# Wider pieces of the expert gate and up weights: 4 contraction blocks by 512 columns

## The chip, the cores and the metric

One core of a Trainium2 chip runs the whole program. The metric is device time in microseconds (us), the median of several runs; lower is better. All data is float32. TensorE does the matmuls, VectorE (DVE) and ScalarE (ACT) work on tiles, GpSimd (POOL) does little here, and SyncE (SP) issues nearly all loads.

## The reference

A decoder of two layers over 256 tokens of width 1024. What matters here is the second layer's mixture of experts, 8 experts of inner width 2816, two chosen for each token:

```python
def swiglu(h, w_gate, w_up, w_down):
    return (jax.nn.silu(h @ w_gate) * (h @ w_up)) @ w_down

def moe_ffn(h, w_router, w_gate, w_up, w_down):
    ...
    logits = (hf @ w_router).astype(jnp.float32)
    top_vals, top_idx = lax.top_k(logits, TOP_K)
    top_w = jax.nn.softmax(top_vals, axis=-1)
    gates = jnp.einsum('nk,nke->ne', top_w, jax.nn.one_hot(top_idx, N_EXPERTS, dtype=jnp.float32))
    out = jnp.zeros_like(hf)
    for e in range(N_EXPERTS):
        out = out + gates[:, e:e + 1].astype(hf.dtype) * swiglu(hf, w_gate[e], w_up[e], w_down[e])
    return out.reshape(B, S, D)
```

Before it stand, in each layer, a norm, an input projection, three groups of token mixers and an output projection; the first layer has one dense SwiGLU of the same inner width. A last norm closes the trunk.

## The kernel before

**Precision.** A float32 operand is split into a high part (`hi`, what ScalarE's copy to the matmul type keeps) and a low part (`lo`, the rest, by a subtraction on VectorE). A product is three matmuls, high by high, high by low, low by high: `mm3`, lines 1394 to 1398, which is why nearly every matmul of the profile stands at L1396, L1397 or L1398.

**Pieces.** All large weights pass in pieces of 1 MB, 128 partitions by 2048 numbers (`PIECE`). SyncE loads a piece into a raw slot. ScalarE writes its high part into `hi_ring` and VectorE its low part into `lo_ring`; both rings have three slots (`SPLIT`). In the expert part there are 11 raw slots: `raw_a` (4) and `raw_m` (7). Semaphores tie them: a raw slot is loaded again when its low part is made (`lo_ready`), a ring slot is written again when TensorE has used the piece before in it (`piece_used`), and TensorE waits for `lo_ready` ahead of each piece.

**Items.** An expert is an item; with up to 128 tokens each, 8 to 11 items run (here 8; the first is written out, the rest are a loop). `gather` (L1678) brings the item's tokens, transposed, into `sel_hi` and `sel_lo` (parts of the tiles `hT_hi` and `hT_lo`) by matmuls with a one-hot matrix. Then 33 pieces follow in the order `ORDER` (lines 116 to 125): G0 U0, then for strips 1 to 10 Gc Uc D(c-1), and D10 last. A strip is `FC` = 256 of the 2816 inner columns. A gate (G) or up (U) piece holds all 8 contraction blocks (`KT`) by 256 columns: 24 matmuls with 128x128 of the tokens stationary and 128x256 of weights moving. Gate and up of a strip share one PSUM bank, `bank[c % 2]`, a half each:

```python
o = bank[c % 2][:, 0:FC] if kind == "G" else bank[c % 2][:, FC:2 * FC]
for k in range(KT):
    ...
    r = mm3(o, sel_hi[:, k, :], sel_lo[:, k, :], wh[:, k, :], wl[:, k, :], k == 0, k == KT - 1)
```

A down (D) piece is 2 contraction blocks by 1024 columns: 12 matmuls with 512 moving columns into banks 4 and 5, which accumulate over the whole item.

**Between them.** After Uc ScalarE makes `m_sg` = Silu of the gate half (L895) and VectorE `m_prod` = up times `m_sg` (L1356). Behind G(c+1) TensorE transposes the two blocks of `m_prod` (`transpose_act`, L1698) into bank 2 or 3; ScalarE copies them to `m_hi` (L905), VectorE makes `m_lo` (L1361), and D(c) uses both. The last strip's transposes stand behind D9, ahead of the next item's gather.

**Order on ScalarE and VectorE.** Their loop `item` goes over the pieces j = 0 to 32: first the split of piece j+2 (`split_expert`, L631 and L935), then what belongs to piece j. At an item's end ScalarE copies banks 4 and 5 to `y_hi` (L910) and VectorE makes `y_lo` (L1379). The next item adds this to `x`: `scatter` (L1690, L1691, four matmuls each behind U0 and behind G1) and `scatter_add` on VectorE (L1340, two each). The one-hot matrix of the current item is transposed behind G2 (L1735).

## Time and profile before

| | |
|---|---|
| median of 3 runs | 1342.34 us (1341.87 to 1343.02) |
| span of the profiled execution | 1337.6 us |
| between the span and the median | 4.7 us |
| TensorE busy | 1278.1 us, 96% |
| VectorE, ScalarE busy | 1022.3 us (76%), 832.6 us (62%) |
| read from HBM | 342.67 MB |

The profile is one execution. Its span runs from the first to the last instruction; for the profiled execution itself no other time is listed, so the time around the span is taken from the median. The expert part begins with the first gather at 503 us and goes on to the end. Times in rows are microseconds from the span's start, unless marked ns. PE is TensorE, PEld its loads of the stationary operand. Matmuls are pipelined, so one matmul's duration is longer than the distance from its start to the next one's: the distance is what the stream costs.

### The profile page before, as it was taken

The page shows a single profiled execution, that of the slowest core. Times are in us where ns is not written, and L with a number is a line of the kernel's source. Part 1 is how long each engine was busy: PE and PEld are TensorE (multiplying, and loading weights), DVE is VectorE, ACT ScalarE, POOL GpSimd, SP SyncE. Part 2 cuts the span into 40 slices and gives each one's busy share as a digit, 9 for nine tenths or more (in the row PEclk, how much of TensorE's full clock was granted, in tenths as well). Part 3 has the DMA queues.
Part 4 walks back from the last instruction along what each step waited for, and adds up shares of the span by engine and source line. Part 5 has one row for each costly group of instructions (what it writes and reads, how often), then busy time and mean ns, then how long its engine had stood idle before and what let it go on. Part 6 is the DMA issues. An engine that isn't in the chain of part 4 may idle for free.

```text
span 1337.6 us, 22912 instructions
## 1 busy us (share of the span) xinstructions
PE 1278.1 (96%) x8754; PEld 1170.5 (88%) x8754; DVE 1022.3 (76%) x1163; ACT 832.6 (62%) x957; POOL 117.4 (9%) x121
## 2 busy tenths in 40 slices
PE   6898899999899789999999999999999999999997
PEld 6876799999787669999999999999999999999996
DVE  5885654455598658888888888888888888888885
ACT  5356544444545656777776776776776777776774
POOL 2850000000086010000000000000000000000000
PEclk9889999999998988999999999999999999999998
DMA  9400665556442069999999999999999999999960
GB/s 326 157 5 1 229 197 183 185 188 189 138 127 71 1 212 366 357 361 304 355 359 307 354 363 299 359 356 306 352 360 303 355 352 320 344 349 324 344 209 31
DMA packets 256650, 344.47 MB, mean 258 GB/s; under 512 B 5558, under 2 KB 227316, under 8 KB 256596
## 3 DMA queue, kind: packets, MB, share of 16 engines
q1 hardware_dynamic: 255772, 341.27, 76.2%
q0 software_dynamic: 624, 1.93, 0.4%
q8 instruction: 35, 0.57, 0.2%
q10 hardware_dynamic: 200, 0.54, 0.1%
q14 instruction: 19, 0.16, 0.0%
HBM read 342.67 MB, written 1.05 MB: 257 GB/s over the span
## 4 chain that ended last, share of the span: by engine, by line
PE 87%; DVE 7%; ACT 3%; issue 2%; DMA 0%; SPq 0%; POOL 0%; POOLq 0%; DVEq 0%; ACTq 0%
PE bank L1396 26%; PE bank L1398 26%; PE bank L1397 26%; PE bank L1678 3%; PE bank L1698 1%; DVE cv L1051 1%; PE bank L1493 1%; DVE lo_ring L930 1%; DVE xn L1051 1%; PE bank L1690 1%; ACT hi_ring L625 1%; PE bank L1691 1%; PE bank L1533 1%; DVE s_sb L1109 0%; DVE q_m L1084 0%
## 5 line engine op out<-in xcount | busy, mean ns | idle before, releaser
L1396 PE MATMUL bank<-hi_ring,hT_hi 128*128 128x256 f32 (+2 forms) x1536 | 449.4, 293 | 0.0
L1397 PE MATMUL bank<-lo_ring,hT_hi 128*128 128x256 f32 (+2 forms) x1536 | 440.7, 287 | 0.0
L1398 PE MATMUL bank<-hi_ring,hT_lo 128*128 128x256 f32 (+2 forms) x1536 | 440.7, 287 | 0.0
L935 DVE TENSOR_TENSOR lo_ring<-raw_m,hi_ring 128x2048 fp32r<-128x2048 f32 x168 | 384.3, 2291 | 60.0 <-ACT hi_ring L631 59.5
L631 ACT ACTIVATE hi_ring<-raw_m 128x2048 fp32r<-128x2048 f32 x168 | 321.0, 1911 | 26.3 <-PE bank L1398 26.3
L1396 PEld LDWEIGHTS bank<-hi_ring,hT_hi 128*128 128x128 f32 x1536 | 293.6, 191 | 8.1 <-issue 1.3
L1397 PEld LDWEIGHTS bank<-lo_ring,hT_hi 128*128 128x128 f32 x1536 | 293.8, 191 | 7.3 <-issue 0.5
L1398 PEld LDWEIGHTS bank<-hi_ring,hT_lo 128*128 128x128 f32 x1536 | 293.7, 191 | 2.7
L935 DVE TENSOR_TENSOR lo_ring<-raw_a,hi_ring 128x2048 fp32r<-128x2048 f32 x96 | 219.4, 2292 | 40.1 <-ACT hi_ring L631 40.1
L930 DVE TENSOR_TENSOR lo_ring<-raw_a,hi_ring 128x2048 fp32r<-128x2048 f32 (+2 forms) x59 | 131.8, 2236 | 93.8 <-ACT hi_ring L625 93.7
L631 ACT ACTIVATE hi_ring<-raw_a 128x2048 fp32r<-128x2048 f32 x96 | 183.4, 1911 | 16.3 <-PE bank L1398 16.3
L1396 PE MATMUL bank<-hT_hi,hi_ring 128*128 128x256 f32 (+1 forms) x576 | 165.2, 287 | 2.2 <-DVE hT_lo L965 2.2
L1397 PE MATMUL bank<-hT_lo,hi_ring 128*128 128x256 f32 (+1 forms) x576 | 163.7, 284 | 0.0
L1398 PE MATMUL bank<-hT_hi,lo_ring 128*128 128x256 f32 (+1 forms) x576 | 163.7, 284 | 0.0
L625 ACT ACTIVATE hi_ring<-raw_a 128x2048 fp32r<-128x2048 f32 (+2 forms) x59 | 109.9, 1863 | 68.9 <-PE bank L1398 62.5
L1396 PE MATMUL bank<-hi_ring,m_hi 128*128 128x512 f32 x352 | 139.4, 396 | 0.0
L1397 PE MATMUL bank<-lo_ring,m_hi 128*128 128x512 f32 x352 | 139.0, 395 | 0.0
L1398 PE MATMUL bank<-hi_ring,m_lo 128*128 128x512 f32 x352 | 139.0, 395 | 0.0
L1396 PEld LDWEIGHTS bank<-hT_hi,hi_ring 128*128 128x128 f32 (+1 forms) x576 | 110.2, 191 | 3.2 <-issue 2.6
L1397 PEld LDWEIGHTS bank<-hT_lo,hi_ring 128*128 128x128 f32 (+1 forms) x576 | 110.3, 191 | 0.5
L1398 PEld LDWEIGHTS bank<-hT_hi,lo_ring 128*128 128x128 f32 (+1 forms) x576 | 110.1, 191 | 0.0
L554 POOL TENSOR_TENSOR rstd<-ms,half_neg 128x1 f32<-128x1 f32 x10 | 6.0, 600 | 1159.4 <-DVE ms L940 1159.4
(266 smaller groups left out, 1457.8 us busy)
## 6 DMA issues: line engine op xcount, KB each, us to landing
raw_m<-in_w_down_exp SPq DMA_DIRECT2D x64, 1024.0 KB, 6.0
raw_m<-in_w_up_exp SPq DMA_DIRECT2D x56, 1024.0 KB, 6.6
raw_m<-in_w_gate_exp SPq DMA_DIRECT2D x48, 1024.0 KB, 5.6
raw_a<-in_w_gate_exp SPq DMA_DIRECT2D x40, 1024.0 KB, 6.4
raw_a<-in_w_up_exp SPq DMA_DIRECT2D x32, 1024.0 KB, 6.8
raw_a<-in_w_down_exp SPq DMA_DIRECT2D x24, 1024.0 KB, 5.2
raw_a<-in_w_in SPq DMA_DIRECT2D x12, 1024.0 KB, 7.1
raw_a<-in_w_gate_dense SPq DMA_DIRECT2D x11, 1024.0 KB, 5.4
```

Of the source, the lines that this page charges most:

```text
L625: A(hi_of(n)[:, 0:w], t[:, 0:w], ACT.Copy).then_inc(hi_ready, 1)
L631: A(hi_of(NA + j), t, ACT.Copy).then_inc(hi_ready, 1)
L930: V.tensor_tensor(lo_of(n)[:, 0:w], raw_slot(n)[0][:, 0:w], hi_of(n)[:, 0:w].bitcast(F32), ALU.subtract).then_inc(lo_ready, 1)
L935: V.tensor_tensor(lo_of(NA + j), expert_slot(i, j)[0], hi_of(NA + j).bitcast(F32), ALU.subtract).then_inc(lo_ready, 1)
L1051: conv(V.scalar_tensor_tensor(out, win, wc, old, ALU.mult, ALU.add))
L1396: M(o, lh, rh, start=start, stop=False)
L1397: M(o, lh, rl, start=False, stop=False)
L1398: return M(o, ll, rh, start=False, stop=stop)
L1493: r = M(bank[1 + r3][0:QD, hh * T:(hh + 1) * T], w_uq[:, c, h * QD:(h + 1) * QD], cq[:, c, :], start=c == 0, stop=c == 1)
L1533: r = nc.tensor.transpose(bank[T_BANK[k % 2]][:, b * P:(b + 1) * P], e_sb[:, k % 3, 0, b * P:(b + 1) * P], ident)
L1678: r = M(bank[b0 + h][:, kk * P:(kk + 1) * P], src[:, t, k * P:(k + 1) * P], onehot[:, t, :], start=t == 0, stop=t == TT - 1)
L1690: M(b[:], onehot_t[:, t, :], y_hi[:, n * 512:(n + 1) * 512], start=True, stop=False)
```

## The change

The expert part gets an order and a strip width of its own. A strip is `EW` = 512 columns, so there are `EC` = 6 strips, five of 512 and one of 256 (2816 = 5 x 512 + 256). A gate or up piece of a 512 strip holds 4 of the 8 contraction blocks by 512 columns; a strip has two of each (`part` 0 and 1), which accumulate into the same bank. The last strip's gate and up are one piece each, with 8 blocks by 256 columns as before. A down piece keeps its form; a 512 strip has two. There are 33 pieces of 1 MB as before, in the order G0 G0 U0 U0, then G G U U D D for strips 1 to 4, then G5 U5 D4 D4 D5. A gate or up piece of a 512 strip is loaded in rows of 2 KB, half as many as before.

Gate goes to bank 0 and up to bank 1, for every strip. The next strip's gate waits for the Silu of this one, its up for the product. Silu stands behind the last gate piece instead of behind the up piece. `m_sg` and `m_prod` have one buffer each, 512 wide, in the tile `xn`, which is free then. Transposes, their copy and their low part are four blocks at a time. The four scatter matmuls that stood behind U0 and behind G1 stand behind the first piece of each, the one-hot transposes behind the first piece of U2, and VectorE makes the next one-hot matrix behind the first piece of D2 instead of behind U5.

```diff
+EW = 2 * FC
+EC = (FF + EW - 1) // EW
...
+    def up(kind, c):
+        return [(kind, c, part) for part in range(expert_width(c) // FC)]
+
+    def down(c):
+        return [("D", c, part) for part in range(expert_width(c) // FC)]
+
+    order = up("G", 0) + up("U", 0)
+    for c in range(1, EC):
+        order += up("G", c) + up("U", c) + down(c - 1)
+    return order + down(EC - 1)
...
-        m_sg = sb("m_sg", [P, 2, FC])
-        m_prod = sb("m_prod", [P, 2, FC])
-        m_hi = sb("m_hi", [P, 2, 2, P], F32R)
-        m_lo = sb("m_lo", [P, 2, 2, P], F32R)
+        m_hi = sb("m_hi", [P, 2, 4, P], F32R)
+        m_lo = sb("m_lo", [P, 2, 4, P], F32R)
...
+        m_sg, m_prod = spare[:, 0:EW], spare[:, EW:2 * EW]
...
-                        src = w[one, :, c * FC:(c + 1) * FC].rearrange("e (k p) n -> p (e k) n", p=P)
-                    sp.dma_start(ff_view(t, kind), src).then_inc(s, 16)
+                        rows = PIECE // expert_width(c) * P
+                        src = w[one, part * rows:(part + 1) * rows, c * EW:c * EW + expert_width(c)
+                                ].rearrange("e (k p) n -> p (e k) n", p=P)
+                    sp.dma_start(expert_view(t, kind, c), src).then_inc(s, 16)
...
-                    if kind == "U":
-                        act.wait_ge(piece_used, expert_done(i, "U", c))
-                        act.wait_ge(prod_done, GU0 + c - 1 + i * NCH)
-                        A(m_sg[:, c % 2, :], bank[c % 2][:, 0:FC], ACT.Silu).then_inc(sg_done, 1)
+                    w = expert_width(c)
+                    if kind == "G" and last_part(kind, c, part):
+                        act.wait_ge(piece_used, expert_done(i, "G", c))
+                        act.wait_ge(prod_done, GU0 + c + i * EC)
+                        A(m_sg[:, 0:w], bank[0][:, 0:w], ACT.Silu).then_inc(sg_done, 1)
...
-                        if c >= 2:
-                            dve.wait_ge(act_t, c - 1 + i * NCH)
-                        V.tensor_tensor(m_prod[:, c % 2, :], bank[c % 2][:, FC:2 * FC], m_sg[:, c % 2, :],
-                                        ALU.mult).then_inc(prod_done, 1)
+                    if kind == "U" and last_part(kind, c, part):
+                        dve.wait_ge(sg_done, GU0 + c + 1 + i * EC)
+                        dve.wait_ge(piece_used, expert_done(i, "U", c))
+                        dve.wait_ge(act_t, c + i * EC)
+                        V.tensor_tensor(m_prod[:, 0:w], bank[1][:, 0:w], m_sg[:, 0:w], ALU.mult).then_inc(prod_done, 1)
...
-                        if kind == "G" and c >= 2:
-                            pe.wait_ge(prod_done, GU0 + c - 1 + i * NCH)
-                        o = bank[c % 2][:, 0:FC] if kind == "G" else bank[c % 2][:, FC:2 * FC]
-                        for k in range(KT):
+                        if part == 0 and c >= 1:
+                            if kind == "G":
+                                pe.wait_ge(sg_done, GU0 + c + i * EC)
+                            else:
+                                pe.wait_ge(prod_done, GU0 + c + i * EC)
+                        o = bank[0 if kind == "G" else 1][:, 0:w]
+                        for kk in range(PIECE // w):
+                            k = part * (PIECE // w) + kk
...
-                    if kind == "G" and c >= 1:
+                    if kind == "G" and c >= 1 and last_part(kind, c, part):
                         transpose_act(i, c - 1)
-                    if not first and c <= 1 and kind == ("U", "G")[c]:
+                    if not first and c <= 1 and kind == ("U", "G")[c] and part == 0:
                         scatter(i, 2 * c)
                         scatter(i, 2 * c + 1)
```

How the rows stand on two engines. First ScalarE in the first item (its loop over the pieces), before: a bit more than one strip. L631 is the split of a weight piece, L895 Silu, L905 the copy of the transposes.

```order
L631 ACTIVATE hi_ring<-raw_a 128x2048 [waits piece_used,raw_in0]
L905 ACTIVATE m_hi<-bank 128x256 [waits piece_used,act_t]
L631 ACTIVATE hi_ring<-raw_a 128x2048 [waits piece_used,raw_in1]
L895 ACTIVATE m_sg<-bank 128x256 [waits prod_done,piece_used]
L631 ACTIVATE hi_ring<-raw_a 128x2048 [waits piece_used,raw_in2]
L631 ACTIVATE hi_ring<-raw_a 128x2048 [waits piece_used,raw_in3]
L905 ACTIVATE m_hi<-bank 128x256 [waits piece_used,act_t]
L631 ACTIVATE hi_ring<-raw_m 128x2048 [waits piece_used,raw_in4]
L895 ACTIVATE m_sg<-bank 128x256 [waits prod_done,piece_used]
```

The same engine with the change, one strip of the first item; L664 is the split, L929 Silu (it writes into `xn`), L940 the copy.

```order
L664 ACTIVATE hi_ring<-raw_m 128x2048 [waits piece_used,raw_in8]
L929 ACTIVATE xn<-bank 128x512 [waits prod_done,piece_used]
L940 ACTIVATE m_hi<-bank 128x512 [waits piece_used,act_t]
L664 ACTIVATE hi_ring<-raw_m 128x2048 [waits piece_used,raw_in9]
L664 ACTIVATE hi_ring<-raw_m 128x2048 [waits piece_used,raw_in10]
L664 ACTIVATE hi_ring<-raw_a 128x2048 [waits piece_used,raw_in0]
L664 ACTIVATE hi_ring<-raw_a 128x2048 [waits piece_used,raw_in1]
L664 ACTIVATE hi_ring<-raw_a 128x2048 [waits piece_used,raw_in2]
L664 ACTIVATE hi_ring<-raw_a 128x2048 [waits piece_used,raw_in3]
L929 ACTIVATE xn<-bank 128x512 [waits prod_done,piece_used]
```

Silu and the copy, which alternated between splits, now stand together, once in six splits, and are twice as wide. Second TensorE in the loop, before: the last matmuls of U0, the scatter, the first of G1.

```order
L1396 MATMUL bank<-hi_ring,hT_hi 128x256
L1397 MATMUL bank<-lo_ring,hT_hi 128x256
L1398 MATMUL bank<-hi_ring,hT_lo 128x256
L1690 MATMUL bank<-hT_hi,onehot_t 128x512 [waits ylo_done0]
L1691 MATMUL bank<-hT_lo,onehot_t 128x512
L1690 MATMUL bank<-hT_hi,onehot_t 128x512 [waits ylo_done1]
L1691 MATMUL bank<-hT_lo,onehot_t 128x512
L1704 REGISTER_ALU
L1396 MATMUL bank<-hi_ring,hT_hi 128x256 [waits lo_ready]
```

With the change: the last matmuls of the first piece of U0, the scatter, the first of its second piece.

```order
L1432 MATMUL bank<-hi_ring,hT_hi 128x512
L1433 MATMUL bank<-lo_ring,hT_hi 128x512
L1434 MATMUL bank<-hi_ring,hT_lo 128x512
L1726 MATMUL bank<-hT_hi,onehot_t 128x512 [waits ylo_done0]
L1727 MATMUL bank<-hT_lo,onehot_t 128x512
L1726 MATMUL bank<-hT_hi,onehot_t 128x512 [waits ylo_done1]
L1727 MATMUL bank<-hT_lo,onehot_t 128x512
L1739 REGISTER_ALU
L1432 MATMUL bank<-hi_ring,hT_hi 128x512 [waits lo_ready]
```

The scatter stood behind two pieces of the item and now stands behind three; the matmuls around it are twice as wide and half as many.

## Rows read from the trace of the kernel before

**Rows 1.** The page: busy time by engine; granted TensorE clock in 40 slices

```profile
PE 1278.1 (96%) x8754; PEld 1170.5 (88%) x8754; DVE 1022.3 (76%) x1163; ACT 832.6 (62%) x957; POOL 117.4 (9%) x121
...
PEclk9889999999998988999999999999999999999998
```

**Rows 2.** Waits, 500 to 1330 us: waiter <- releaser: us, times, longest

```profile
DVE lo_ring L935 <- ACT hi_ring L631: 99.6, 216, 1.2
ACT m_hi L905 <- PE bank L1698: 95.0, 80, 2.6
...
PE bank L1663 <- DVE chosen L1279: 2.3, 1, 2.3
...
PE bank L1690 <- DVE hT_lo L1379: 1.4, 1, 1.4
```

**Rows 3.** Windows: length, busy us by engine, clock, DMA share, GB/s

```profile
620.00:700.00 80.00, 80.00 (x567) 74.88 (x566) 70.03 (x53) 56.91 (x46) 0.00 (x0) 1.00 1.04 352
604.55:706.52 101.97, 101.97 (x725) 95.53 (x724) 87.01 (x66) 72.41 (x62) 0.00 (x0) 1.00 1.01 340
706.52:808.49 101.97, 101.97 (x726) 95.53 (x724) 87.13 (x66) 72.40 (x62) 0.00 (x0) 1.00 1.01 341
```

**Rows 4.** Order of time, TensorE at an item's start: start, us, engine, line

```profile
713.11 0.28 PE L1396 MATMUL bank<-hi_ring,hT_hi 128*128 128x256 f32 x1
...
718.86 0.40 PE L1690 MATMUL bank<-hT_hi,onehot_t 128*128 128x512 f32 x1
...
719.79 0.28 PE L1396 MATMUL bank<-hi_ring,hT_hi 128*128 128x256 f32 x1
```

**Rows 5.** Order of time, TensorE in two strips: transposes, a down piece, transposes

```profile
700.64 0.38 PE L1698 MATMUL bank<-consts,m_prod 128*128 128x128 f32 x2
...
700.98 0.28 PE L1397 MATMUL bank<-lo_ring,hT_hi 128*128 128x256 f32 x1
...
703.72 0.39 PE L1396 MATMUL bank<-hi_ring,m_hi 128*128 128x512 f32 x1
...
706.52 0.38 PE L1698 MATMUL bank<-consts,m_prod 128*128 128x128 f32 x2
```

**Rows 6.** Order of time, TensorE in a down piece of the dense layer

```profile
301.92 0.39 PE L1396 MATMUL bank<-hi_ring,d_hi 128*128 128x512 f32 x1
...
305.81 0.39 PE L1398 MATMUL bank<-hi_ring,d_lo 128*128 128x512 f32 x1
```

**Rows 7.** Groups by line and form, 500 to 1330 us: busy us, mean ns

```profile
L935 DVE TENSOR_TENSOR lo_ring<-raw_m,hi_ring 128x2048 fp32r<-128x2048 f32 x168 | 384.3, 2291 | 60.0 <-ACT hi_ring L631 59.5
L631 ACT ACTIVATE hi_ring<-raw_m 128x2048 fp32r<-128x2048 f32 x168 | 321.0, 1911 | 26.3 <-PE bank L1398 26.3
...
L1356 DVE TENSOR_TENSOR m_prod<-bank,m_sg 128x256 f32<-128x256 f32 x88 | 36.8, 418 | 0.0
...
L1379 DVE TENSOR_TENSOR hT_lo<-bank,hT_hi 128x512 fp32r<-128x512 f32 x16 | 10.3, 686 | 23.6 <-ACT hT_hi L910 23.6
...
L910 ACT ACTIVATE hT_hi<-bank 128x512 fp32r<-128x512 f32 x16 | 8.7, 596 | 17.9 <-PE bank L1398 17.9
```

**Rows 8.** Order of time, ScalarE and VectorE at the same item's start

```profile
714.28 3.82 ACT L631 ACTIVATE hi_ring<-raw_a 128x2048 fp32r<-128x2048 f32 x2
...
716.22 4.49 DVE L935 TENSOR_TENSOR lo_ring<-raw_a,hi_ring 128x2048 fp32r<-128x2048 f32 x2 [1.00 <-ACT hi_ring L631]
...
719.14 0.39 ACT L895 ACTIVATE m_sg<-bank 128x256 f32<-128x256 f32 x1 [1.04 <-PE bank L1398]
```

**Rows 9.** Loads issued from 620 to 640 us: count, KB, us to landing

```profile
raw_m<-in_w_gate_exp SPq DMA_DIRECT2D x2, 1024.0 KB, 5.8
```

**Rows 10.** Loads issued from 680 to 700 us

```profile
raw_m<-in_w_gate_exp SPq DMA_DIRECT2D x2, 1024.0 KB, 7.5
```

More of the change, by code:

```diff
@@ L504, in expert_loads @@
             def expert_loads(e, i, first):
-                for j, (kind, c) in enumerate(ORDER):
+                for j, (kind, c, part) in enumerate(E_ORDER):
                     if first and j < RAW_A:
@@ L884, in item @@
             def item(i, more):
-                for j, (kind, c) in enumerate(ORDER):
+                for j, (kind, c, part) in enumerate(E_ORDER):
                     if j + 2 < NFF or more is True:
@@ L1343, in item @@
             def item(i, more, first=False):
-                for j, (kind, c) in enumerate(ORDER):
+                for j, (kind, c, part) in enumerate(E_ORDER):
                     if j + 2 < NFF or more is True:
@@ L1724, in item @@
                                 pe.wait_ge(gathered, 3 + k // 4 + 4 * i)
-                            r = mm3(o, sel_hi[:, k, :], sel_lo[:, k, :], wh[:, k, :], wl[:, k, :], k == 0, k == KT - 1)
+                            r = mm3(o, sel_hi[:, k, :], sel_lo[:, k, :], wh[:, kk, :], wl[:, kk, :],
+                                    k == 0, k == KT - 1)
                     r.then_inc(piece_used, 1)
-                    if kind == "G" and c >= 1:
+                    if kind == "G" and c >= 1 and last_part(kind, c, part):
@@ L1728, in item @@
                         transpose_act(i, c - 1)
-                    if not first and c <= 1 and kind == ("U", "G")[c]:
+                    if not first and c <= 1 and kind == ("U", "G")[c] and part == 0:
                         scatter(i, 2 * c)
                         scatter(i, 2 * c + 1)
-                    if kind == "G" and c == 2:
+                    if kind == "U" and c == 2 and part == 0:
                         pe.wait_ge(x_upd, XU0 + 4 * i)
```

69 lines of the change are left out of this document (41 added, 28 removed).

## The prediction, made before the changed kernel ran

> **What bounds the kernel now.** I read the engine line of the profile's page first, then the waits of the expert part, then the windows of single items, and last the order of time inside one item. The engine line has TensorE busy for 96% of the span, and the clock line shows full speed nearly everywhere from the middle on [rows 1]. In the waits of the expert part TensorE hardly appears: its longest are 2.3 us once at the routing and 1.4 us once at a scatter, while VectorE and ScalarE wait a hundred times for ScalarE and for TensorE [rows 2]. The two windows, each cut from the transposes of an item's last strip to the same place one item later, are 101.97 us long both times, with TensorE busy for all of it at clock 1.00 [rows 3]. So the eight items cost what the matmul stream costs, and everything else has to stay ahead of it. The reader should see that "busy" alone would not prove this; the absence of waits and the even pitch of the rows do.
>
> The stream's pitch is in the order of time. Gate and up of a first strip are 48 matmuls of 256 columns from 713.11 to 718.86: 5.75 us, 0.1198 us each, 2.875 us a piece [rows 4]. A down piece is 12 matmuls of 512 columns from 703.72 to 706.52: 2.80 us, 0.2333 us each [rows 5]. Two transposes take 0.22 us: from 700.64 to 700.98 there are 0.34 us, in which one 0.12 us matmul lies too [rows 5]. I check this against the window: 22 x 2.875 + 11 x 2.80 + 11 x 0.22 = 96.5, and 5.5 us remain for 32 gather matmuls, 8 scatter matmuls (0.93 us per four [rows 4]) and the one-hot transposes. It closes.
>
> **The change, part by part.** (1) *Wider matmuls.* In an item 20 of the 22 gate and up pieces change from 24 matmuls of 256 columns to 12 of 512; the last strip is 256 wide, and its two pieces keep their shape. The new form is that of the down pieces: moving rows of 512 from a ring slot, a 128x128 stationary operand, a whole bank written. So a piece falls from 2.875 to 2.80 us: 0.075 x 20 = 1.5 us an item, 8 items in this run, 12.0 us. Nothing overlaps this, since it is the stream that sets the end. The lower end of the price is the same 512 form in the dense layer, 17 matmuls from 301.92 to 305.81, 0.2288 us each [rows 6]: a piece would be 2.746 us, and the gain 0.129 x 160 = 20.6 us. The upper end is twice the 256 pitch, no gain. I take 0.2333, since it was measured in this loop, at its load of DMA.
>
> On what the pitch is made of: from the two rows, 2 x 0.1198 - 0.2333 = 6.3 ns are won for each pair of matmuls joined. The Trainium skill, "TensorE: Matmul & The Clock Gate", section "Back-to-back issue gap", gives an isolated warm gap of columns over 2.4 GHz plus 2.5 ns. By that rule a joined pair would win only 2.5 ns, 4.8 us in all (an estimate from the page); the rows of this trace stand at twice that, and the sum goes by the rows. The same section has about 131 ns for 512 columns in a stream with weight loads; the row's 233 ns disagree, and the measurement decides.
>
> (2) *Transposes.* Ten strips had two transposes each, behind the next strip's gate piece, and the eleventh two before the gather; now five strips have four each and the sixth two: 22 in both. At 0.11 us each nothing changes [rows 5].
>
> (3) *ScalarE and VectorE.* Of Silu, product and the two splits of the activation there are 6 each instead of 11, five of them twice as wide. A 256-wide one is 0.42 us on VectorE, a 512-wide one 0.69 (the y split has that form); the 512-wide ScalarE copy is 0.60 [rows 7]. Over an item VectorE has 22 x 0.42 = 9.2 us of them before and 10 x 0.69 + 2 x 0.42 = 7.7 after, ScalarE 22 x 0.39 [rows 8] = 8.6 before and 10 x 0.60 + 2 x 0.39 = 6.8 after. Neither is on the path, so this gives 0, but where the wide ones stand matters.
>
> (4) *The ring.* The ring of split weights has three slots. The split of piece j+2 can begin when piece j-1 is used; it takes 1.91 us on ScalarE, then 2.29 on VectorE [rows 7], and must be there 5.6 us after piece j started. The tightest place of a strip is behind the second gate piece, where Silu (moved here from behind the up piece) and the copy of the four transposes now follow each other. With 0 at the end of that piece's stream: Silu starts at 0.28 (719.14 against 718.86 [rows 4, 8]) and ends at 0.9, the copy ends at 1.5, the weight split on ScalarE runs to 3.4, that on VectorE to 5.7; VectorE's own low part of the activation fits between. The piece is due at 0.44 + 2 x 2.80 = 6.04, so 0.3 us are left. At the item's start the third piece is due at 713.11 + 5.60 = 718.71, since the scatter that stood before it is now behind it; VectorE ended the first of its two splits at 716.22 + 2.29 = 718.51 [rows 8]: 0.2 us left. The scatter's two additions on VectorE now stand behind the split of piece 4, and piece 4 is due after 4 x 2.80 + 0.93 us; 1 us and more is left there. So the ring costs 0 in the forecast, with 0 to 0.1 us an item as its bound at the item's start.
>
> (5) *Single banks.* Gate always goes to bank 0 and up to bank 1, and each new strip waits for the Silu and the product of the last. Silu ends 0.9 us behind gate, and the next gate begins more than 11 us behind it. The product follows the last up piece by a VectorE split at most (some 3 us), and the next up strip begins four pieces later. What queues behind these waits on TensorE is the whole stream, but they are met long before: 0. The product is also due at the next transposes, two down and two gate pieces later instead of one and one.
>
> (6) *Loads.* A gate or up megabyte is 512 rows of 2 KB instead of 1,024 of 1 KB; issues and slots stay. DMA has some share in this: between 620 and 700 us its engines are busy for 1.04 and move 352 GB/s [rows 3], while a gate load's time to landing grows from 5.8 to 7.5 us within the item [rows 9, 10]. So it falls behind a little in the strips and catches up in the gather. A slot is loaded 11 pieces ahead and split 2 ahead of use, some 9 x 2.9 = 26 us after its issue, which covers 7.5. At 352 GB/s 33 pieces need 98.3 us, less than the 100.5 us of a new item. The gain of longer rows falls where nothing waits: 0.
>
> **Sum.** An item goes from 101.97 to 100.45 us; 8 x 1.5 = 12.0. From this I take 0.3 us for the first microseconds of item 0 at the low clock and small stalls: 11.7. The span of 1337.6 us goes to 1325.9. What lies between the span and the median of the runs, 4.7 us, stays: 1330.6 us.
>
> **Rivals.** *The dense pitch* (0.2288 us): 1342.3 - 20.6 = 1321.7. For it, the same form shows it; against it, the loop's own rows do not, not even at the busiest or the quietest place. *Half the gain*: the 6.3 ns of a joined pair compare two kinds of piece with different stationary operands, so part of them may belong to the down piece and not to the width. With 3.2 ns a pair, 240 pairs an item and 8 items, 6 us are won: 1336.4. For it, each row is one kind only; against it, both pitches hold evenly over whole pieces. The rule of the Trainium skill quoted above ("TensorE: Matmul & The Clock Gate") would put the time at 1337.5, an estimate from the page. *DMA becomes the bound*: if what DMA moved in an item (340 GB/s [rows 3]) were all it could move, the item would stay at 101.97 us and the time at 1342. Against it speaks the 352 GB/s of the strips and the lag that is made up. *The ring falls behind*, the one that ends slower: behind the second gate piece VectorE delivers the split later than I work out, because Silu, copy and low part are wider. Its price is 40 strips times what exceeds 0.3 us. If each 512-wide operation took twice a 256-wide one, the 0.3 would just be used up, 1331; at 0.6 us late the gain is gone; at 0.8 us late it is 40 x 0.5 - 11.7 = +8, 1350.6. For it speaks that VectorE is busy for 87 of 102 us; against it, that the 512-wide rows are measured.
>
> **Chances.** The forecast 0.69; the dense pitch 0.12; half the gain 0.08; DMA 0.04; the ring 0.07. The range takes in the forecast, most of the dense pitch and half the gain, and leaves out the ring and DMA: 1322 to 1337. A measurement of this kernel can tell about 0.2%, 2.7 us, from no change. Faster by more than that: forecast, dense pitch and nearly all of the half gain, 0.88; same 0.05 (DMA and the rest of it); slower 0.07.
>
> **What would show it.** Right: gate and up rows of 128x512 at a start-to-start of 0.233 us; an item window of 100.4 to 100.5 us with TensorE busy throughout; no row in which TensorE waits for the low ring; loads landing sooner than 7.5 us late in an item. The ring's slip would show as TensorE idle before the first down piece of each strip with VectorE's split as releaser, and as VectorE no longer waiting for ScalarE. DMA as the bound would show as ScalarE waiting for a raw slot. A pitch of 0.229 us would mean the dense price. I am wrong if the 512 form with this stationary operand has another pitch than the down pieces, or if the split durations grow.

## The result, and the profile after

| | median | runs | lowest, highest |
|---|---|---|---|
| before | 1342.11 us | 4 | 1339.68, 1343.02 |
| changed | 1321.09 us | 4 | 1318.69, 1321.78 |

The ratio is 0.9846, with an interval of 0.9834 to 0.9858. The change wins 21.0 us where the forecast had 11.7, and the time lies 0.9 us below the lower end of the range. The profiled execution of the changed kernel took 1321.78 us with a span of 1320.0, so 1.8 us lie around the span. The page of the changed kernel, its span, its engine line, its clock line and its DMA line, to be read beside [rows 1]:

```profile
span 1320.0 us, 18637 instructions
PE 1260.0 (95%) x6834; PEld 1070.5 (81%) x6834; DVE 1011.0 (77%) x1083; ACT 828.8 (63%) x877; POOL 117.7 (9%) x121
...
PEclk9899999999899797999999999999999999999998
...
DMA packets 174725, 344.40 MB, mean 261 GB/s; under 512 B 5558, under 2 KB 63476, under 8 KB 174676
```

TensorE has 1920 matmuls fewer (240 an item, 8 items) and is still the engine that is always busy. Windows of the changed kernel, columns as in [rows 3]: the same 80 us, and two items, cut from gather to gather.

```profile
620.00:700.00 80.00, 80.00 (x385) 66.53 (x384) 71.20 (x46) 57.88 (x39) 0.00 (x0) 1.00 1.00 359
604.77:704.30 99.53, 99.53 (x487) 82.88 (x486) 85.75 (x56) 71.95 (x52) 0.00 (x0) 1.00 0.97 349
704.30:803.76 99.46, 99.46 (x487) 82.88 (x486) 85.68 (x56) 71.92 (x52) 0.00 (x0) 1.00 0.97 349
```

An item went from 101.97 to 99.46 us, 2.51 less, where 1.5 was forecast. TensorE fills it as before, at clock 1.00. From the first gather to the last the stretch went from 815.35 to 796.54 us, 18.8 less: seven items at 2.5, and the first, which begins at a lower clock, at 1.3 (101.58 to 100.28). The two executions differ in how long that clock lasted; the window from 511 to 515 us, columns as in [rows 3], before and after:

```profile
511.00:515.00 4.00, 4.00 (x31) 4.00 (x31) 2.84 (x12) 2.46 (x2) 0.00 (x0) 0.85 1.06 367
```

```profile
511.00:515.00 4.00, 4.00 (x12) 3.23 (x12) 2.85 (x36) 2.40 (x2) 0.00 (x0) 0.50 1.05 387
```

The granted clock was 0.50 from 502.0 to 512.2 us before and from 502.3 to 516.0 us after, so 9.1 us of the first item passed at it before and 11.5 us after; at half the clock 2.4 us more cost 1.2 us (an estimate from these rows), which is what the first item gained less. What stands ahead of the first gather was 1.4 us longer in this execution (504.49 against 503.11) and the tail 0.2 shorter, so the span is 17.6 us shorter than the span shown before.

The pitch, in the changed kernel's order of time on TensorE (columns as in [rows 4]): two gate or up pieces and two down pieces.

```profile
675.43 0.39 PE L1432 MATMUL bank<-hi_ring,hT_hi 128*128 128x512 f32 x1
676.11 0.39 PE L1432 MATMUL bank<-hi_ring,hT_hi 128*128 128x512 f32 x1
...
680.88 0.60 PE L1734 MATMUL bank<-consts,xn 128*128 128x128 f32 x4
681.23 0.48 PE L1432 MATMUL bank<-hi_ring,hT_hi 128*128 128x512 f32 x1
...
686.80 0.39 PE L1432 MATMUL bank<-hi_ring,m_hi 128*128 128x512 f32 x1
...
692.39 0.28 PE L1432 MATMUL bank<-hi_ring,hT_hi 128*128 128x256 f32 x1
```

This is the surprise. From 675.43 to 680.88 there are 24 matmuls with `hT_hi` and `hT_lo` as the stationary operand: 5.45 us, **0.2271 us** each. From 686.80 to 692.39 there are 24 of the same form, same ring, same 512 columns, with `m_hi` and `m_lo`: 5.59 us, **0.2329 us** each. So [rows 5] gave the right price for the down pieces, and the wrong one for the pieces that the change made. [rows 5] and [rows 6] were not all that the trace of the kernel before had on this form. In the output projection of its trunk, `hT_hi` and `hT_lo` are the stationary operand of 512-wide matmuls too:

```profile
478.98 0.39 PE L1396 MATMUL bank<-hi_ring,hT_hi 128*128 128x512 f32 x1
...
488.05 0.39 PE L1397 MATMUL bank<-lo_ring,hT_hi 128*128 128x512 f32 x1
```

40 distances in 9.07 us, **0.2268 us** each: the very form of the new pieces, with the same stationary tile and ring, at the pitch that they came to have. I had not read these rows. Two questions follow: does the width alone carry the gain, and what makes one stationary tile 6 ns dearer than the other?

Where the other work went, in groups of the changed kernel from 490 to 1320 us (columns as in [rows 7]):

```profile
L1391 DVE TENSOR_TENSOR xn<-bank,xn 128x512 f32<-128x512 f32 x40 | 27.4, 684 | 0.0
...
L929 ACT ACTIVATE xn<-bank 128x512 f32<-128x512 f32 x40 | 24.0, 599 | 40.2 <-PE bank L1434 40.1
L940 ACT ACTIVATE m_hi<-bank 128x512 fp32r<-128x512 f32 x40 | 23.8, 594 | 0.1
```

And the waits in the same stretch (columns as in [rows 2]):

```profile
ACT hi_ring L664 <- PE bank L1434: 140.6, 183, 2.6
DVE lo_ring L970 <- ACT hi_ring L664: 92.1, 159, 2.2
...
PEld bank L1432 <- DVE lo_ring L970: 2.4, 8, 0.4
```

TensorE's weight load waits for the low ring once an item, 0.3 us. The place is the third piece of an item; TensorE and VectorE there, in order of time:

```profile
715.95 0.39 PE L1434 MATMUL bank<-hi_ring,hT_lo 128*128 128x512 f32 x1
716.21 0.50 PE L1432 MATMUL bank<-hi_ring,hT_hi 128*128 128x512 f32 x1
716.54 0.40 PE L1433 MATMUL bank<-lo_ring,hT_hi 128*128 128x512 f32 x1
716.78 0.40 PE L1434 MATMUL bank<-hi_ring,hT_lo 128*128 128x512 f32 x1
```

```profile
713.86 4.49 DVE L970 TENSOR_TENSOR lo_ring<-raw_a,hi_ring 128x2048 fp32r<-128x2048 f32 x2 [1.00 <-ACT hi_ring L664]
```

The first of the two splits ends at 713.86 + 2.29 = 716.15, and the piece starts at 716.21. Two distances are 0.26 and 0.33 us where 0.227 is the rule: 0.13 us are lost in each item, though nearly all of it is hidden in "busy".

### The profile page after: what moved, and what is told of

Same layout as the page of the kernel before. It is cut to its first block, busy times and chain, and to the rows that moved or that the text cites. A ratio compares the mean times of both kernels' runs of the same rounds, so it can differ in the third digit from the quotient of the medians.

```text
span 1320.0 us, 18637 instructions
## 1 busy us (share of the span) xinstructions
PE 1260.0 (95%) x6834; PEld 1070.5 (81%) x6834; DVE 1011.0 (77%) x1083; ACT 828.8 (63%) x877; POOL 117.7 (9%) x121
## 3 DMA queue, kind: packets, MB, share of 16 engines
HBM read 342.67 MB, written 1.05 MB: 260 GB/s over the span
## 4 chain that ended last, share of the span: by engine, by line
PE 87%; DVE 7%; ACT 3%; issue 2%; DMA 0%; SPq 0%; POOL 0%; POOLq 0%; DVEq 0%; ACTq 0%
PE bank L1432 26%; PE bank L1434 26%; PE bank L1433 26%; PE bank L1714 3%; PE bank L1734 1%; DVE cv L1086 1%; PE bank L1529 1%; DVE lo_ring L965 1%; DVE xn L1086 1%; ACT hi_ring L658 1%; PE bank L1569 1%; PE bank L1726 1%; PE bank L1727 1%; PE bank L1511 0%; DMA vec_rows<-in_diff_subln 0%
## 5 line engine op out<-in xcount | busy, mean ns | idle before, releaser
L664 ACT ACTIVATE hi_ring<-raw_m 128x2048 fp32r<-128x2048 f32 x168 | 322.2, 1919 | 84.6 <-PE bank L1434 84.6
L1432 PE MATMUL bank<-hi_ring,hT_hi 128*128 128x512 f32 (+2 forms) x896 | 336.3, 375 | 0.0
L1434 PE MATMUL bank<-hi_ring,hT_lo 128*128 128x512 f32 (+2 forms) x896 | 329.6, 368 | 0.0
L1433 PE MATMUL bank<-lo_ring,hT_hi 128*128 128x512 f32 (+2 forms) x896 | 329.0, 367 | 0.0
L664 ACT ACTIVATE hi_ring<-raw_a 128x2048 fp32r<-128x2048 f32 x96 | 183.4, 1918 | 57.5 <-PE bank L1434 57.5
L1432 PEld LDWEIGHTS bank<-hi_ring,hT_hi 128*128 128x128 f32 x896 | 169.6, 189 | 30.6 <-DVE lo_ring L970 2.4
L1434 PEld LDWEIGHTS bank<-hi_ring,hT_lo 128*128 128x128 f32 x896 | 169.4, 189 | 28.7
L1433 PEld LDWEIGHTS bank<-lo_ring,hT_hi 128*128 128x128 f32 x896 | 169.7, 189 | 27.4 <-issue 0.5
```

Of the source, the lines that this page charges most:

```text
L664: A(hi_of(NA + j), t, ACT.Copy).then_inc(hi_ready, 1)
L1432: M(o, lh, rh, start=start, stop=False)
L1433: M(o, lh, rl, start=False, stop=False)
L1434: return M(o, ll, rh, start=False, stop=stop)
```

## The experiments

Two theories to begin with. **Placement**: the 6 ns belong to the address of the stationary tile in SBUF relative to that of the ring, both taken modulo 256 bytes. These places are the start addresses that the built program gives its tiles. As built, both rings start at 128, `hT_hi` and `hT_lo` at 128, and `m_hi` and `m_lo` at 96 in both kernels. **Order**: they belong to how the down pieces run, two banks in turn with one stationary block used for both. Some expectations number the forms of the placement theory, each in its own way: in before_hshift the numbers stand for how the cost would go over to 256-wide matmuls, in rel128 and best2 A2 is that only the relation to the ring counts and A3 that the stationary tile's own place does. In all of the experiments the distance from the first gather matmul of one item to that of the next (the item, below) is read from the profile to within 0.02 us, and it carries a verdict where one time cannot.

**w256: all of the change but the width.** Pieces, order, loads, banks, Silu and transposes as changed; each 512-wide matmul is written as two of 256.

```diff
-                            r = mm3(o, sel_hi[:, k, :], sel_lo[:, k, :], wh[:, kk, :], wl[:, kk, :],
-                                    k == 0, k == KT - 1)
+                            for h in range(w // FC):
+                                cols = slice(h * FC, (h + 1) * FC)
+                                r = mm3(o[:, cols], sel_hi[:, k, :], sel_lo[:, k, :], wh[:, kk, cols], wl[:, kk, cols],
+                                        k == 0 and h == 0, k == KT - 1 and h == w // FC - 1)
```

> The changed kernel with each gate and up matmul of 512 columns made as two of 256; order, banks, loads, Silu, product and transposes as in the change. Theory (all of the gain is the width of the matmul): gate and up go back to 0.1198 us a matmul, an item to 101.97 us, and the time to that of the kernel before, within 2 us. Rival (a part of the 21 us comes from the order, the banks, the loads or the moved scatter): the item stays clearly under 101.97 us, e.g. 101 us, and the time under 1337 us.

Measured: 1342.19 us, ratio 1.001 (1.000 to 1.002) to 1341.09 for the kernel before. Its item:

```profile
605.70:707.76 102.06, 102.06 (x728) 95.62 (x726) 86.17 (x56) 71.92 (x52) 0.00 (x0) 1.00 0.95 340
```

102.06 against 101.97 us [rows 3]: parts (2) to (6) of the prediction together cost 0.09 us an item as long as the pieces are no faster, and the width brings the whole gain, 102.06 - 99.46 = 2.60 us an item. No weight load waits for the low ring here, so the 0.13 us of the third piece belong to the faster stream (hshift below shows the same). The DMA share falls from 1.01 to 0.95 with it, and nothing comes of that.

**align: `m_hi` and `m_lo` moved by 32 bytes**, to 128, the rings' place. Nothing else is touched.

```diff
+        shift = sb("shift", [P, 8])
         m_hi = sb("m_hi", [P, 2, 4, P], F32R)
```

> The changed kernel with 32 bytes put before m_hi, so that m_hi and m_lo begin at a multiple of 64 bytes as hT_hi, hT_lo do; nothing else. Theory A (the place of the stationary tile makes the down pieces' 0.2333 us against 0.2268 of gate and up): the down pieces fall to 0.227, an item by 132 x 0.0065 = 0.86 us, the time by 6.9 us to 1314. Rivals (banks, neighbours in time, load of DMA make it): no change, 1321.

Measured: 1315.46 us, ratio 0.9808 (0.9792 to 0.9825), 5.6 us below the changed kernel. Its item, and a pair of down pieces:

```profile
705.31:804.00 98.69, 98.69 (x487) 82.93 (x486) 85.69 (x56) 71.94 (x52) 0.00 (x0) 1.00 0.97 350
```

```profile
736.06 0.39 PE L1433 MATMUL bank<-hi_ring,m_hi 128*128 128x512 f32 x1
...
741.50 0.39 PE L1433 MATMUL bank<-hi_ring,hT_hi 128*128 128x512 f32 x1
```

24 down matmuls now take 5.44 us, 0.2267 each, like the gate pieces. An item is 0.79 us shorter (98.67): 132 down matmuls at 6.3 ns would be 0.83.

**d_sel: the down pieces of strips 0 to 4 take `sel_hi` and `sel_lo` as stationary operand**, in the order and banks of the down pieces. The kernel then leaves the activations out of these pieces.

```diff
-                                r = mm3(bank[4 + n][:], m_hi[:, c % 2, ff, :], m_lo[:, c % 2, ff, :],
+                                lh, ll = (m_hi[:, c % 2], m_lo[:, c % 2]) if c == EC - 1 else (sel_hi, sel_lo)
+                                r = mm3(bank[4 + n][:], lh[:, ff, :], ll[:, ff, :],
```

> The down pieces of strips 0 to 4 take the gathered tokens (sel_hi, sel_lo) as stationary operand instead of m_hi, m_lo; waits as before; the output is not the reference's. Theory A (it is the stationary tile): these down pieces run at 0.227 us. Rival B (it is the change between banks 4 and 5, or what runs beside them): they stay at 0.2333 us.

Measured: one time, 1313.29 us, and an item of 98.74 us. Same instructions, same banks, other tile: the item of align within 0.07 us, and its last down piece, 12 matmuls at 6 ns, still used `m_hi` and `m_lo`. Order cannot explain it.

**d_nouter: the down pieces bank by bank** instead of two banks in turn.

```diff
-                        for f in range(2):
-                            for n in range(2):
+                        for n in range(2):
+                            for f in range(2):
```

> The down piece's loops exchanged: 6 matmuls into bank 4, then 6 into bank 5, instead of 3 and 3 twice. Rival B (the change of banks costs): fewer changes, the mean of a down piece falls from 0.2333 to between 0.227 and 0.231 us. Theory A (stationary tile): unchanged at 0.2333 us.

Measured: one time, 1321.49 us, and an item of 99.46 us, that of the changed kernel to the hundredth. The order theory falls.

**hshift: the other way round, `hT_hi` and `hT_lo` moved 32 bytes away from the ring's place.** The second pad moves everything behind by 64 bytes in all; `m_hi` comes to 160, again not the ring's place.

```diff
+        pad1 = sb("pad1", [P, 8])
         hT_hi = sb("hT_hi", [P, KT, T], F32R)
         hT_lo = sb("hT_lo", [P, KT, T], F32R)
+        pad2 = sb("pad2", [P, 8])
```

> The changed kernel with hT_hi and hT_lo (where sel_hi and sel_lo lie) moved by 32 bytes, so that they begin 32 bytes off a multiple of 64, and 32 bytes behind them; m_hi and m_lo stay 32 off as they were. Theory A (a stationary tile 32 bytes off a multiple of 64 costs 6.5 ns a matmul of 512 columns): gate and up rise from 0.2268 to 0.2333 us, an item from 99.46 to 101.0, the expert part by 12.5 us, to about 1334 if the trunk, whose moving operand this tile is, does not change. Rival (only m_hi's own part of memory is slow): no change in the expert part, 1321.

Measured: one time, 1326.89 us. Its item, and a pair of gate or up pieces:

```profile
703.14:803.65 100.51, 100.51 (x487) 82.95 (x486) 85.68 (x56) 71.94 (x52) 0.00 (x0) 1.00 0.95 346
```

```profile
739.87 0.40 PE L1434 MATMUL bank<-hi_ring,hT_hi 128*128 128x512 f32 x1
...
745.47 0.60 PE L1736 MATMUL bank<-consts,xn 128*128 128x128 f32 x4
```

24 gate or up matmuls take 5.60 us, 0.2333 each: the pitch follows the address, and the price of the prediction is exactly what the change costs in this layout. The item is 1.05 us longer than in the changed kernel, where I expected 1.5: the first matmuls of each run of pieces are as slow in the right place (see before_align), the third piece no longer waits (the weight loads wait for the low ring for 0.3 us in the whole run instead of 2.4), and the 256-wide pieces are a little faster (see before_hshift). What no theory had foreseen is that the first gather came at 501.6 us, 2.9 us sooner. In nine profiles in which the trunk's tiles keep their relation (before, changed, w256, align, align64, d_sel, d_nouter, before_align, rel128) it came between 502.9 and 507.0 us, so the size of such a difference is not to be trusted; its sign is borne out by the pitches below.

**align64: `m_hi` and `m_lo` moved by 96 bytes**, to 192 (the pad of align with 24 instead of 8).

> The changed kernel with 96 bytes put before m_hi: it begins at 64 past a multiple of 128. If a multiple of 64 is enough, down pieces run at 0.227 us and the time is that of the run with 32 bytes, 1315. If only a multiple of 128 is fast, they lie higher: 0.229 us, as the dense layer's down pieces, whose tile lies like this (1317.5), or 0.2333 (1321).

Measured: one time, 1321.74 us, item 99.56 us, and a pair of down pieces from 734.43 to 740.03, 5.60 us. 64 bytes off are as bad as 32: it is not enough that the tile stands at a multiple of 64.

**before_align: the pad of align in the kernel before.** `m_hi` and `m_lo` come to 128, the width of gate and up stays 256.

> The kernel before with 32 bytes put before m_hi, nothing else. Theory A: its down pieces fall from 0.2333 to 0.2268 us, an item from 101.97 to 101.1, the time by 6.9 us to 1334. Then aligned down pieces of the kernel before would have given the right price of the changed gate and up pieces. Rival: the ring or the loads hold the item at 101.97, 1341.

Measured: 1337.67 us, ratio 0.9972 (0.9962 to 0.9982) to 1341.27. A down piece in the order of time on TensorE:

```profile
747.85 0.40 PE L1397 MATMUL bank<-hi_ring,m_hi 128*128 128x512 f32 x1
...
750.60 0.28 PE L1397 MATMUL bank<-hi_ring,hT_hi 128*128 128x256 f32 x1
```

2.75 us where [rows 5] had 2.80. The item is 0.52 us shorter (101.45) where I expected 0.86. The reason stands in the rows of one piece: the first five or so matmuls behind transposes or behind a change of width take 0.228 to 0.236 us, 0.232 in the mean, also in the right place, and here each down piece follows a change of width. In the changed kernel down pieces come in pairs behind 512-wide ones.

**before_hshift: the pads of hshift in the kernel before.**

> The kernel before with hT_hi and hT_lo moved by 32 bytes: its gate and up matmuls of 256 columns then have a stationary tile 32 bytes off. Theory A1 (the cost goes with the matmul): 0.1263 us, 528 x 8 x 0.0065 = 27 us more, 1368. A2 (it goes with the columns that pass): half, 1355. A3 (a 256-wide matmul is bound by something else and hides it): 1341.

Measured: one time, 1331.18 us, outside of all that was expected. The first gather is at 499.7 us, 3.4 us sooner, and the item is 101.39 us instead of 101.97. Both come mainly from 256-wide matmuls. In the loop, gate and up ones with the tile away from the ring's place take 0.1185 us instead of 0.1196. In the dense layer, where the ring is the stationary operand and `hT_hi` the moving one, the change is larger; windows from 200 to 300 us of before_hshift and of the changed kernel, whose trunk is that of the kernel before:

```profile
200.00:300.00 100.00, 100.00 (x722) 94.25 (x721) 50.56 (x43) 42.39 (x43) 0.00 (x0) 1.00 0.59 189
```

```profile
200.00:300.00 100.00, 100.00 (x707) 94.13 (x706) 50.28 (x42) 42.03 (x42) 0.00 (x0) 1.00 0.58 189
```

Both are full and at clock 1.00; one holds 722 matmuls, the other 707. The 256-wide ones stand at 0.1167 us there instead of 0.1200. So the wide matmul wants its tiles at the same place, and the narrow one is a little faster when they are 32 bytes apart. In the trunk's 3.4 us three parts meet, each an estimate from the rows of these profiles: 1728 matmuls of 256 columns at 3.3 ns win up to 5.7 us, 264 with `d_hi` or `d_lo`, which the pads moved to the ring's place, win 0.4 (0.2291 to 0.2277 us over whole pieces), and 192 of 512 columns with `hT` as the stationary operand lose 1.3 (0.2268 to 0.2334 us).

That also corrects the value of the change itself: with `hT` out of place it is worth much less. The single times differ by 1331.18 - 1326.89 = 4.3 us, and the stretch from the first gather to the last, which leaves out the trunk, by 6.1 us (810.7 to 804.6; item 101.39 to 100.51), where with `hT` in place it is 18.8.

**two_views: one tile that serves the trunk at 32 bytes from the ring's place and the experts at a multiple of 128.** For the experts high part at 128, low part at 0, for the trunk 160 and 32; `m_hi`, `m_lo` and `d_hi` at 0 modulo 256. Pads ahead of `d_hi` and `m_hi`, and the merging of small tiles, are left out here.

```diff
-        hT_hi = sb("hT_hi", [P, KT, T], F32R)
-        hT_lo = sb("hT_lo", [P, KT, T], F32R)
+        hT_t = sb("hT", [P, 2 * (KT * T + 32) - 24], F32R)
+        hT_hi_t, hT_lo_t = hT_t[:, 0:KT * T + 8], hT_t[:, KT * T + 32:2 * KT * T + 40]
+        hT_hi, hT_lo = (t[:, 8:8 + KT * T].rearrange("p (k t) -> p k t", k=KT) for t in (hT_hi_t, hT_lo_t))
...
-        sel_hi = hT_hi[:, 0:4, :].rearrange("p a b -> p (a b)").rearrange("p (k s) -> p k s", k=KT)
+        sel_hi = hT_hi_t[:, 0:D].rearrange("p (k s) -> p k s", k=KT)
...
```

> A version meant to beat both: the changed kernel with m_hi, m_lo and the dense layer's d_hi, d_lo at multiples of 128 bytes, and with one tile for the hT parts, in which the trunk's view begins 32 bytes behind a multiple of 128 and the experts' views (sel, y) at a multiple. Theory (place of the stationary tile decides the 512-wide matmuls, and the trunk's gate and up matmuls of 256 columns fall from 0.120 to 0.117 us when their moving operand is 32 bytes off, as seen with the tile moved): the expert part as in the run with m_hi moved by 32 bytes (item 98.6 us), the trunk about 6 us shorter, 1309 us. Rival (the trunk's gain was run to run noise): 1315.

Measured: 1321.73 us, ratio 0.9851 (0.9834 to 0.9868) to 1340.97, and not the 1309 that I expected. The first gather is at 500.8 us, so the trunk's part came; the item is 100.07 us, 1.4 more than in align. Its down matmuls stand at 0.232, its gate and up ones at 0.231. A multiple of 128 is not enough. The gate and up ones are mixed: from a matmul with `sel_hi` (128) to the next with `sel_hi` the distance is 0.2275 us, from `sel_hi` to `sel_lo` (0) 0.2324, from `sel_lo` to `sel_hi` 0.2339 (means over 472 to 558 distances). So the tile's own place does not set the distance behind it alone; the place of the next one counts too.

**ring32: the rings moved by 32 bytes to 160, `hT` and `m` to 0.**

```diff
+        pad3 = sb("pad3", [P, 8])
         hi_ring = sb("hi_ring", [P, SPLIT, PIECE], F32R)
         lo_ring = sb("lo_ring", [P, SPLIT, PIECE], F32R)
+        pad4 = sb("pad4", [P, 24])
...
+        shift = sb("shift", [P, 8])
         m_hi = sb("m_hi", [P, 2, 4, P], F32R)
```

> The changed kernel with m_hi, m_lo at a multiple of 128 bytes and the two rings moved by 32 bytes: in the experts the moving operand is 32 off and the stationary one at a multiple of 128; in the trunk's gate and up pieces the other way round. If the distance of the two places decides, the experts' 512-wide matmuls fall under 0.2268 us (to 0.223, the item to 97.1) or rise to 0.2333 (101.1); if only the stationary tile's place decides, they stay at 0.2268 (98.6).

Measured: one time, 1332.48 us, item 100.80 us, the longest with 512-wide matmuls. All of them take 0.234 us, with stationary tiles at a multiple of 256. The trunk tells that the gain of 256-wide matmuls is not one of any distance. There the moving `hT` lies 96 bytes from the ring, the 256-wide ones stay at 0.1200 us, and the window that held 722 matmuls in before_hshift holds 704 (`d_hi`, now 32 bytes off, has its share in that):

```profile
200.00:300.00 100.00, 100.00 (x704) 93.68 (x704) 49.77 (x41) 41.64 (x40) 0.00 (x0) 1.00 0.57 187
```

**rel128: everything moved by 128 bytes together**, rings, `hT` and `m` at 0 modulo 256.

```diff
+        pad3 = sb("pad3", [P, 32])
         hi_ring = sb("hi_ring", [P, SPLIT, PIECE], F32R)
...
+        shift = sb("shift", [P, 8])
         m_hi = sb("m_hi", [P, 2, 4, P], F32R)
```

> The changed kernel with 128 bytes put before the rings, and 32 before m_hi: rings, hT_hi, hT_lo, m_hi and m_lo now all begin at a multiple of 256 bytes (in the run with m_hi moved by 32 bytes all of them began 128 past one). Theory A2 (a 512-wide matmul is fast when its moving and its stationary tile have the same place within 256 bytes): item 98.67 us as there, 1315. Theory A3 (the stationary tile must be 128 past a multiple of 256, whatever the moving one does; it fits the runs so far as well): all of them slow at 0.2333 or near, item 100.5 to 101, 1333.

Measured: one time, 1314.82 us. Its item, and a pair of down pieces:

```profile
701.93:800.60 98.67, 98.67 (x488) 82.93 (x486) 85.67 (x56) 71.96 (x52) 0.00 (x0) 1.00 0.97 352
```

```profile
732.66 0.39 PE L1434 MATMUL bank<-hi_ring,m_hi 128*128 128x512 f32 x1
...
738.10 0.39 PE L1434 MATMUL bank<-hi_ring,hT_hi 128*128 128x512 f32 x1
```

5.44 us for 24, and the item of align to the hundredth, with tiles at 0 instead of 128. What counts is the relation of stationary tile and ring, not the place of either; the form of the theory by which the absolute place counts falls. In align the two are an odd multiple of 256 bytes apart and fast, so a period of 512 is out as well.

**best2: two_views with the second view at 2112 numbers, so that `sel_hi`, `sel_lo`, `m_hi`, `m_lo` and `d_hi` are all at 128, the ring's place, while the trunk's `hT` views stay 32 bytes off.** To make room, small tiles are merged.

```diff
+        hT_t = sb("hT", [P, 2112 + KT * T + 8], F32R)
+        hT_hi_t, hT_lo_t = hT_t[:, 0:KT * T + 8], hT_t[:, 2112:2112 + KT * T + 8]
...
+        d_pad = sb("d_pad", [P, 48])
...
+        shift = sb("shift", [P, 32])
```

> A version meant to beat both: the changed kernel with the stationary tiles of the 512-wide matmuls (sel, m, and the dense layer's d) 128 past a multiple of 256 bytes like the rings, and the trunk's view of the hT tile 32 bytes further. Both A2 and A3 expect an item of 98.67 us as in the run with m_hi moved, and a trunk 3 to 6 us shorter than there, since the 256-wide trunk matmuls with this tile moving ran at 0.117 instead of 0.120 us when it was moved by 32 bytes: 1309 to 1312. If the place within 256 bytes is not what matters, the item lies at 99.5 to 100.5 and the time at 1318 to 1326.

Measured: 1308.51 us (1306.24 to 1312.06 in 4 runs), ratio 0.9755 (0.9732 to 0.9779) to 1341.36. The first gather is at 500.05 us. An item of it:

```profile
796.50:895.07 98.57, 98.57 (x488) 82.92 (x486) 85.67 (x56) 72.03 (x52) 0.00 (x0) 1.00 0.97 350
```

It is the best version, 12.6 us below the changed kernel: 0.90 us an item, 7.2 in eight, and the trunk's 4.4 (504.49 to 500.05); that makes 11.6, and 1.0 us is left to the spread of single profiles. Since the first gather alone spreads by 4 us among unchanged trunks, the 4.4 is no measurement of the trunk's part either.

All of it in one table, places in bytes modulo 256, pitches of 512-wide matmuls in the steady part of a piece:

| kernel | ring | `sel_hi`, `sel_lo` | `m_hi`, `m_lo` | gate, up pitch | down pitch | item | time |
|---|---|---|---|---|---|---|---|
| changed | 128 | 128, 128 | 96 | 0.2271 | 0.2329 | 99.46 | 1321.09 |
| align | 128 | 128, 128 | 128 | 0.227 | 0.2267 | 98.67 | 1315.46 |
| rel128 | 0 | 0, 0 | 0 | 0.227 | 0.2267 | 98.67 | 1314.82 |
| best2 | 128 | 128, 128 | 128 | 0.227 | 0.227 | 98.56 | 1308.51 |
| align64 | 128 | 128, 128 | 192 | 0.227 | 0.2333 | 99.56 | 1321.74 |
| two_views | 128 | 128, 0 | 0 | 0.231 | 0.232 | 100.07 | 1321.73 |
| hshift | 128 | 160, 160 | 160 | 0.2333 | 0.233 | 100.51 | 1326.89 |
| ring32 | 160 | 0, 0 | 0 | 0.234 | 0.234 | 100.80 | 1332.48 |

## Why the prediction was right, and where it failed

**What bounds the kernel** was right. The item stayed full of TensorE, and its length followed the pitch of the matmuls in every run.

**(1) Wider matmuls** is the step that failed, by its size. The mechanism, columns per matmul, is shown by w256. The price was wrong: I took 0.2333 us "since it was measured in this loop", as if the loop were what set it. The row was that of another stationary tile, and the 6 ns were this tile's address. The row with this tile stood unread in the same trace (478.98 to 488.05, above). The right price for a piece was 12 x 0.2268 = 2.722 us, not 2.80, and the gain of a piece 0.153 us, not 0.075. That makes 20 x 0.153 = 3.06 us an item; 2.60 were measured (w256 to changed), and the difference of 0.46 is the third piece's 0.13 and some 0.33 for the starts: behind transposes, scatter and gather the first matmuls stay at 0.232. One such start costs 0.03 to 0.05 us, and an item has eight (the 24 matmuls and four transposes from 680.88 to 686.80 take 5.92 us, where 5.45 and 4 x 0.11 would be 5.89).

**The rival "dense pitch"** at 1321.7 came within 0.6 us, and I gave it 0.12. That it came so near is in part luck: its gain of 0.129 us a piece meets the 2.60 / 20 = 0.130 measured, but the pieces run at 0.2268, and what the starts and the third piece take back happens to make up the difference to 0.2288. I set its evidence aside because the loop's own down rows spoke against it; but it was a row of the same form with another stationary tile [rows 6]. Two tiles at two pitches were the sign that the tile is a variable, and the trunk's rows with `hT_hi` would have been the third. Nor did the range hold what it said: it began at 1322, above this rival's own 1321.7, while it was said to take in most of it. The 0.2288 was itself no bound: `d_hi` stands at 64, and with `d_hi` at the ring's place (hshift, best2) the same matmuls take 0.2273. So the lower end of my range, built on it, was too high.

**The rival "half the gain"** had the right question and the wrong sign. I wrote that the 6.3 ns of a joined pair compare two kinds of piece, and that part of them might belong to the down piece. It did: 6.5 ns of it, to its disadvantage. Compared at the same place a pair wins 2 x 0.1198 - 0.2268 = 12.8 ns; compared with both out of place, 2 x 0.1185 - 0.2333 = 3.7 ns, which is before_hshift against hshift. When two rows compared differ in a second thing, the error can be on either side, and the range has to be open on both.

**The 0.3 us taken off for the first item** came out at 1.2 in this pair of profiles, and it hangs on the execution: in d_sel the clock rose at 512.2 us, as in the kernel before.

**What a pitch is made of.** At the same place 0.1198 and 0.2268 us are the columns over 2.4 GHz, 106.7 and 213.3 ns, plus 13.1 and 13.5: a fixed part of 13 ns a matmul, paid half as often. The section "Back-to-back issue gap" of "TensorE: Matmul & The Clock Gate" in the Trainium skill has 2.5 ns for it, for isolated matmuls; this kernel's runs, with a weight load ahead of every matmul, show five times that. By 13 ns the forecast would have been 3.1 us an item, where 2.60 were measured, so nearer than 1.5, and too high by the starts and the third piece. The split holds between these two widths and this placement only: the trunk's 192-wide matmuls take 0.1117 us, 80.0 ns plus 31.7.

**(2) Transposes, (3) ScalarE and VectorE, (5) single banks, (6) loads**: 0 each, and w256 holds them together at 0.09 us an item. The wide operations took what [rows 7] gave: 684 ns on VectorE, 599 and 594 on ScalarE. Between 620 and 700 us DMA has a share of 1.00 and moves 359 GB/s, more than the 352 of [rows 3], for an item that is 2.5 us shorter. The rival in which 340 GB/s were the limit falls with that. Loads issued from 680 to 700 us land in 6.3 to 8.1 us: 6.6 for gate in `raw_m`, sooner than the 7.5 of [rows 10], as forecast, but 8.0 for up and 8.1 for down in the same slots.

**(4) The ring** was placed rightly and its bound was too narrow. At the item's start I had 0.2 us of slack and 0 to 0.1 us as the cost; 0.13 us an item, 1.0 in all, were lost there. The step that failed is again the pitch: with two pieces of 2.72 us instead of 2.80 ahead of it, the third piece is due 0.16 us sooner, and nearly all of the slack is gone. In hshift, where a pair of pieces takes 5.60 us again, the wait is nearly gone (0.3 us in the whole run). A forecast with the faster pitch would have had to say so. The tightest place in a strip, with 0.3 us by my count, shows no wait.

**The time around the span** was a second, smaller slip. I took 4.7 us, the profiled span against the median of the runs. In the runs with both numbers 1.7 to 2.0 us lie around it. The rest, some 3 us, can only be that the profiled execution of before, whose own time is not listed, was a quick one among runs that spread from 1339.7 to 1343.0. It did no harm to the forecast, which is a difference, but it is the wrong name for that offset. With the profile's own 1.8 us the forecast for the changed kernel's profile was 1325.9 + 1.8 = 1327.7, and 1321.8 came.

## What to carry to other kernels

Before you take a price from one kind of instruction for another, list in what they differ beside the thing that you change, the operands' addresses among it, and look for more rows, in other parts of the program too; two rows of one form at two prices say that there is a hidden variable. With weights streamed through a ring and a matmul of 512 columns, try the stationary tiles at the ring's place modulo 256 bytes: a pad of 32 bytes was worth 5.6 us of 1321 here. For 256-wide matmuls try 32 bytes off. When matmuls are joined, write the pitch as columns over the clock plus a fixed part, and take the fixed part from the pitch of the pieces that are changed: [rows 4] alone, 0.1198 - 0.1067 = 13 ns, would have given 240 x 13.1 ns = 3.1 us an item, where 2.6 came.

## What the runs showed of the hardware

- The pitch of a 512-wide matmul depends on where its stationary tile stands relative to its moving tile, modulo 256 bytes: 0.2267 us at the same place (align at 128, rel128 at 0), 0.2329 at 32 bytes before it (changed), 0.2333 at 32 (hshift) and 64 (align64) behind it, 0.232 at 128 (two_views) and 0.234 at 96 behind (ring32). 64 before it, `d_hi` in the trunk, gave 0.2288 [rows 6].
- A 256-wide one goes the other way by less: 0.1196 to 0.1198 at the same place, 0.1185 at 32 bytes off; with the ring as stationary operand 0.1200 at the same place, 0.1167 at 32 bytes off (before_hshift, hshift, best2), and 0.1200 again at 96 (ring32).
- The first five or so 512-wide matmuls behind transposes or behind a change of width take 0.228 to 0.236 us also at the same place (align, before_align).
- Left open: what in the chip does this. The runs give the pitch by place and by width of a stream whose tiles all stand at one place, and no view shows the reads themselves. Whose place counts is open too, the matmul's own tile or the next one's, whose load overlaps it. In the changed kernel the last matmul ahead of a down piece (`hT_lo`, next `m_hi` at 96) takes 0.235 us and the last of a down piece (`m_lo`, next `hT_hi`) 0.2265, as if the next tile paid. In align64, with `m_hi` and `m_lo` at 192, it is the other way round: 0.2257 and 0.2306.
